# w_out's block sums in two buffer sets from their rows' landing; entry of the output stage by 256 tokens

## The reference

```python
h = _rmsnorm(x, g_pre)                                    # x: 1024 tokens x 1024
proj = einsum('bsd,dn->bsn', h, w_in)                     # q,k,v,z of A, q,k,v,z,lr of B, 2 gates
o_sb = stick_breaking(q, k, v)                            # A: 8 heads x 64, strictly causal
y_sb = (o_sb * silu(sb_z)) @ w_o_sb
log_alpha = log_sigmoid(gla_lr @ w_alpha_up + b_alpha_up) / 16
o_gla = _rmsnorm(gla_chunked(q, k, v, log_alpha), g_gla_norm)   # B: 4 heads
y_gla = (o_gla * silu(gla_z)) @ w_o_gla
merged = sigmoid(gA + bA) * y_sb + sigmoid(gB + bB) * y_gla
x = x + merged @ w_out
return _rmsnorm(x, g_final)
```

## Time and profile before

| | us |
|---|---|
| median of 3 runs | 827.39 |
| lowest, highest | 826.4, 827.99 |
| profiled execution | 827.49 |
| its span | 825.2 |
| PE busy | 795.7 (96%) |
| DVE busy | 585.2 (71%) |
| ACT busy | 410.1 (50%) |
| POOL busy | 54.7 (7%) |

### The profile page before, as it was taken

The page is one execution under the profiler, slowest core; times in us unless marked ns, Lnnn a source line. Parts: engine busy times, 40 slices in busy tenths (PEclk is TensorE's granted clock), DMA queues, the critical chain, the costliest instruction groups (busy, mean ns, idle before and its releaser), DMA issues.

```text
span 825.2 us, 11846 instructions
## 1 busy us (share of the span) xinstructions
PE 795.7 (96%) x4441; PEld 664.1 (80%) x4441; DVE 585.2 (71%) x807; ACT 410.1 (50%) x705; POOL 54.7 (7%) x44
## 2 busy tenths in 40 slices
PE   5989999999999999999999999999999999989996
PEld 4767888888788888879889888888888888868785
DVE  6776986989698888965545646566467777775884
ACT  8645665667566565756235245244344333353332
POOL 1550000000000000020000000000000000002510
PEclk9999999999999999999999999999999999999999
DMA  9794102202120220022111010244433334499232
GB/s 318 223 344 152 43 27 52 51 25 51 51 51 26 51 52 27 27 58 60 38 52 27 2 52 26 77 140 153 143 125 103 102 103 123 131 355 357 105 120 85
DMA packets 75171, 84.70 MB, mean 103 GB/s; under 512 B 3932, under 2 KB 57335, under 8 KB 74104
## 3 DMA queue, kind: packets, MB, share of 16 engines
q1 hardware_dynamic: 75074, 84.10, 31.5%
q10 hardware_dynamic: 54, 0.01, 0.0%
HBM read 59.98 MB, written 19.92 MB: 97 GB/s over the span
## 4 chain that ended last, share of the span: by engine, by line
PE 76%; DVE 12%; issue 4%; DMA 4%; ACT 3%; SPq 0%; DVEq 0%; ACTq 0%
PE pj L722 21%; PE ob L974 5%; PE sc L974 5%; PE tr L1026 4%; PE pj L866 4%; PE ob L1026 4%; DVE surv L1700 4%; PE pj L1026 4%; PE ob L814 3%; PE sc L1026 3%; PE tr L824 3%; PE pj L847 3%; PE pj L738 2%; PE sc L791 2%; PE sc L790 2%
## 5 line engine op out<-in xcount | busy, mean ns | idle before, releaser
L722 PE MATMUL pj<-h_hi,w_lo 128*128 128x512 f32 x336 | 134.6, 401 | 0.0
L722 PE MATMUL pj<-h_hi,w_hi 128*128 128x512 f32 x336 | 134.6, 400 | 0.0
L722 PE MATMUL pj<-h_lo,w_hi 128*128 128x512 f32 x336 | 134.3, 400 | 0.0
L1700 DVE TENSOR_TENSOR_SCAN surv<-surv 128x128 f32<-128x128 f32 (+3 forms) x64 | 86.4, 1350 | 24.1 <-ACT beta L1212 23.5
L722 PEld LDWEIGHTS pj<-h_hi,w_lo 128*128 128x128 f32 x336 | 63.9, 190 | 12.3 <-issue 0.5
L722 PEld LDWEIGHTS pj<-h_lo,w_hi 128*128 128x128 f32 x336 | 63.7, 190 | 12.2 <-issue 0.3
L722 PEld LDWEIGHTS pj<-h_hi,w_hi 128*128 128x128 f32 x336 | 63.9, 190 | 11.8 <-issue 0.2
L1253 ACT ACTIVATE wt_hi<-tr 128x512 fp32r<-128x512 f32 (+2 forms) x96 | 43.6, 490 | 43.3 <-PE tr L824 41.7
L1604 DVE TENSOR_TENSOR w_lo<-w_raw,w_hi 128x1024 fp32r<-128x1024 f32 x33 | 40.3, 1221 | 26.8 <-ACT w_hi L1124 26.6
L1745 DVE TENSOR_TENSOR wt_lo<-tr,wt_hi 128x512 fp32r<-128x512 f32 (+2 forms) x96 | 50.0, 548 | 5.3 <-ACT wt_hi L1253 4.8
L1703 DVE TENSOR_TENSOR beta<-beta,surv 128x128 f32<-128x128 f32 (+3 forms) x64 | 48.5, 758 | 2.2
(11 more groups left out here) (397 smaller groups left out, 1939.5 us busy)
## 6 DMA issues: line engine op xcount, KB each, us to landing
w_raw<-in_w_in SPq DMA_DIRECT2D x30, 512.0 KB, 3.7
tw<-w_scratch SPq DMA_DIRECT2D x8, 1024.0 KB, 9.2
y_scratch<-y_ring SPq DMA_DIRECT2D x28, 256.0 KB, 2.1
graw<-in_w_in SPq DMA_DIRECT2D x14, 512.0 KB, 5.2
y_back<-y_scratch SPq DMA_DIRECT2D x14, 512.0 KB, 5.2
x_t<-in_x SPq DMA_DIRECT2D x8, 512.0 KB, 6.6
wrow<-in_w_out SPq DMA_DIRECT2D x4, 1024.0 KB, 6.9
w_scratch<-wsum_h SPq DMA_DIRECT2D x4, 1024.0 KB, 7.6
```

What stands on the lines that cost most here:

```text
L722: mm = pe.matmul(pj[bank][:, :], (w_lo if p == 2 else w_hi)[:, slot, k, :], (h_lo if p == 1 else h_hi)[:, k, HALF * h:HALF * h + HALF], st ...
L1700: dve.tensor_tensor_scan(s[:, ::-1], s[:, ::-1], s[:, ::-1], 1.0, ALU.mult, ALU.bypass)\
```

## The change

In the opening the sums go round in two sets of places (k % 2) and each store has a semaphore of its own. POOL starts k = 0 with the landing of its rows, k = 2 waits for the store of k = 0's low part, and k = 3 for that of k = 1's. ACT's high part of k waits for the store of the high part of k - 2. ACT and DVE split all four before stage_k of c = 4 and before the stack; DVE's stack waits for the stores of the high parts of k = 1 and k = 3, and ACT and DVE enter the pairs when all eight are stored. All eight splits of h's first half stand before the split of k's weights. PE takes v's first half before the low-rank product, with the rounds of turns spread anew. The small loads of w_up go behind load 5.

At the output stage the last gate block is finished in two parts of 256 columns, and the first 256 tokens are merged, then both row blocks are split, then the rest is merged. The broadcast of g_final moves from before POOL's wait for the merge into its first pair, and DVE and ACT wait for it ahead of the first row sum and the first square. The norms of the pair before stand behind the third gather. g_fin_row lies elsewhere, and tw 3 is loaded ahead of x_res.

```diff
-        wsum = [at(f"wsum{k}", kb, [P, 4, HALF]) for k, kb in enumerate((F + 52, F + 68.125, F + 16, F + 52))]
-        wsum_h = [at(f"wsum_h{k}", kb, [P, 4, HALF], F32R) for k, kb in enumerate((F + 8, F + 40, F + 8, 108))]
-        wsum_l = [at(f"wsum_l{k}", kb, [P, 4, HALF], F32R)
-                  for k, kb in enumerate((F + 52, F + 68.125, F + 16, 100))]
+        wsum = [at("wsum0", F + 52, [P, 4, HALF]), at("wsum1", F + 68.125, [P, 4, HALF])]
+        wsum_h = [at("wsum_h0", F + 8, [P, 4, HALF], F32R), at("wsum_h1", F + 40, [P, 4, HALF], F32R)]
+        wsum_l = [at("wsum_l0", F + 52, [P, 4, HALF], F32R), at("wsum_l1", F + 68.125, [P, 4, HALF], F32R)]
...
             load(4, COL_Q + P, 0)
-            for c in range(8):
-                sp.dma_start(w_up[RANK * c:RANK * (c + 1), :], w_alpha_up[0]).then_inc(up_loaded, 16)
             load_wrow(2)
             load_wrow(3)
-            for k in range(3):
+            for k in range(4):
                 for part in range(2):
                     store_wsum(part, k)
             twin(0, 2)
             load(5, COL_K + P, 1)
-            for part in range(2):
-                store_wsum(part, 3)
-            for n, stores in enumerate((32, 32, 32, 16, 16)):
-                sp.wait_ge(wsum_stored[n], stores)
+            for c in range(8):
+                sp.dma_start(w_up[RANK * c:RANK * (c + 1), :], w_alpha_up[0]).then_inc(up_loaded, 16)
+            for n in range(2 * 4):
+                sp.wait_ge(wsum_stored[n], 16)
...
             load_tw(2)
-            sp.wait_ge(m_step, 3 * NP + 2)
-            load_res(0)
             sp.wait_ge(prod_done, NP * NP)
             load_tw(3)
+            sp.wait_ge(m_step, 3 * NP + 5)
+            load_res(0)
...
-            pool.wait_ge(x_normed, ST)
             for k in range(4):
                 top, low = wrow[k % 2][:, 0, :], wrow[k % 2][:, 1, :]
-                ts = wsum[k]
+                ts = wsum[k % 2]
                 pool.wait_ge(wrow_loaded[k % 2], 16 * (k // 2) + 16)
-                if k == 2:
-                    pool.wait_ge(tr_ready, R0)
-                if k == 3:
-                    pool.wait_ge(wsum_stored[0], 32)
+                if k >= 2:
+                    pool.wait_ge(wsum_stored[2 * k - 3], 16)
...
-            pool.wait_ge(fin_loaded, 16)
-            pool.partition_broadcast(g_fin[:, :], g_fin_row[0:1, :], P).then_inc(fin_bc, 1)
-
             pool.wait_ge(m_ready, 2)
-            pool.wait_ge(m_step, 3 * NP + 2)
+            pool.wait_ge(m_step, 3 * NP + 5)
...
                 if p == 1:
+                    pool.wait_ge(fin_loaded, 16)
+                    pool.partition_broadcast(g_fin[:, :], g_fin_row[0:1, :], P).then_inc(fin_bc, 1)
                     pool.wait_ge(o5_ready, 4)
...
             pe.wait_ge(cols_ready, 2)
             first_tile(0, 0, 0, [(7, 3)])
             first_tile(1, 1, 0, [])
+            first_tile(2, 2, 0, [(8, 4), (9, 6)])
             for k in range(KT):
-                turn_x([KT + k] if k < 3 else [])
+                turn_x([10 + k // 3] if k % 3 == 0 else [])
                 low_rank(0, k)
-            first_tile(2, 2, 0, [(11, 0), (12, 2), (13, 4), (14, 6)])
-            turn_x([15])
-            for n in range(2):
-                first_tile(n, 3 + n, 1, [])
+            first_tile(0, 3, 1, [(13, 0), (14, 1), (15, 3)])
+            first_tile(1, 4, 1, [])
             first_tile(2, 5, 1, [])
             for k in range(KT):
                 low_rank(1, k)
...
                 if o == 0 and p == 1:
-                    pe.wait_ge(comb, 5 * NP)
+                    pe.wait_ge(comb, 5 * NP + 1)
                     pe.wait_ge(sig_a, 2 * NP)
...
             def wsum_high(k, half):
 
                 hs = slice(2 * half, 2 * half + 2)
                 act.wait_ge(wsum_done, 4 * k + 4)
-                if k == 2:
-                    act.wait_ge(wsum_stored[0], 32)
-                act.activation(wsum_h[k][:, hs, :], wsum[k][:, hs, :], ACT.Copy).then_inc(wsum_hi, 1)
-
+                if k >= 2:
+                    act.wait_ge(wsum_stored[2 * k - 4], 16)
+                act.activation(wsum_h[k % 2][:, hs, :], wsum[k % 2][:, hs, :], ACT.Copy).then_inc(wsum_hi, 1)
+
+            for half in range(2):
+                wsum_high(0, half)
+            h_high(range(KT, KT + 2))
+            wsum_high(1, 0)
+            stage(v_t, 2, 0, 0)
+            wsum_high(1, 1)
+            h_high(range(KT + 2, KT + 5))
             lr_quarters(0)
-            h_high([KT + 3])
-            wsum_high(0, 0)
-            h_high([KT + 4])
-            wsum_high(0, 1)
             h_high(range(KT + 5, R0))
-            stage(v_t, 2, 0, 0)
             for half in range(2):
-                wsum_high(1, half)
+                wsum_high(2, half)
             stage(stage_q, 3, 1, 1)
             for half in range(2):
-                wsum_high(2, half)
+                wsum_high(3, half)
             stage(stage_k, 4, 1, 0)
             act.wait_ge(proj_free, 5)
-            act.wait_ge(wsum_stored[1], 32)
             for part in range(2):
                 stack(0, part)
             high_part(3, 1, 2, proj_ready, 5)
-            wsum_high(3, 0)
             stage(v_t, 5, 1, 1)
-            wsum_high(3, 1)
             lr_quarters(1)
-            act.wait_ge(wsum_lo, 8)
-            act.wait_ge(wsum_stored[2], 32)
-            act.wait_ge(wsum_stored[3], 16)
+            for n in range(2 * 4):
+                act.wait_ge(wsum_stored[n], 16)
...
                                bias=cols[:, 17 + v:18 + v]).then_inc(sig_b, 1)
+
+            def finish_part(part, done):
+
+                ps = slice(256 * part, 256 * part + 256)
+                act.wait_ge(comb, done)
+                act.activation(gates2[:, 1, ps], gates2[:, 1, ps], ACT.Sigmoid,
+                               bias=cols[:, 16 + NP:17 + NP]).then_inc(sig_b, 1)
 
...
-            finish_b(NP - 1)
+            finish_part(0, 5 * NP)
+            finish_part(1, 5 * NP + 1)
...
                     if o < 3:
                         act.wait_ge(prod_done, NP * NP)
-                        act.wait_ge(m_step, 3 * NP + 2)
+                        act.wait_ge(m_step, 3 * NP + 5)
                     if o == 3:
-                        act.wait_ge(fin_bc, 1)
+                        act.wait_ge(wout_l, 3)
...
             for o in range(4):
                 high_out(1, o)
+            act.wait_ge(fin_bc, 1)
             act.wait_ge(o5_free, 3)
             square(0, 0)
...
+            wsum_low(0, 0)
+            h_low(range(KT, KT + 2))
+            wsum_low(0, 1)
+            stage(v_t, 2, 0, 0)
+            wsum_low(1, 0)
+            h_low(range(KT + 2, KT + 5))
             lr_quarters(0)
-            h_low(range(KT + 3, KT + 5))
-            wsum_low(0, 0)
-            h_low([KT + 5])
-            wsum_low(0, 1)
-            h_low(range(KT + 6, R0))
-            stage(v_t, 2, 0, 0)
+            h_low(range(KT + 5, R0))
+            wsum_low(1, 1)
             for half in range(2):
-                wsum_low(1, half)
+                wsum_low(2, half)
             stage(stage_q, 3, 1, 1)
             for half in range(2):
-                wsum_low(2, half)
+                wsum_low(3, half)
             stage(stage_k, 4, 1, 0)
-            dve.wait_ge(wsum_stored[1], 32)
+            dve.wait_ge(wsum_stored[2], 16)
+            dve.wait_ge(wsum_stored[6], 16)
             for part in range(2):
                 stack(0, part, part)
             low_part(3, 1)
             stage(v_t, 5, 1, 1)
-            dve.wait_ge(proj_ready, 6)
-            for half in range(2):
-                wsum_low(3, half)
             lr_quarters(1)
-            dve.wait_ge(wsum_stored[2], 32)
-            dve.wait_ge(wsum_stored[3], 16)
+            for n in range(2 * 4):
+                dve.wait_ge(wsum_stored[n], 16)
...
-                dve.wait_ge(sig_a, 2 * v + 2)
-                dve.wait_ge(back_loaded, 32 * v + 32)
-                dve.tensor_tensor(mT[:, KT - 2 - v, :], s_a, y_back[:, 0, :], ALU.mult).then_inc(m_step, 1)
                 if v + 1 < NP:
+                    dve.wait_ge(sig_a, 2 * v + 2)
+                    dve.wait_ge(back_loaded, 32 * v + 32)
+                    dve.tensor_tensor(mT[:, KT - 2 - v, :], s_a, y_back[:, 0, :], ALU.mult).then_inc(m_step, 1)
                     low_item(v + 1, 5)
-                last_block(v)
-
-
-            def merge_last(h, done):
-
-                hs = slice(HALF * h, HALF * h + HALF)
-                dve.wait_ge(sig_b, 2 * NP - h)
-                dve.tensor_tensor(s_b[:, hs], s_b[:, hs], y_back[:, 1, hs], ALU.mult).then_inc(m_step, 1)
-                dve.wait_ge(m_step, 3 * NP - 2 + done)
-                dve.tensor_tensor(mT[:, 0, hs], mT[:, 0, hs], s_b[:, hs], ALU.add).then_inc(m_step, 1)
-
-            merge_last(1, 1)
-            merge_last(0, 3)
+                    last_block(v)
+
+
+            def last_part(part):
+
```

(78 more changed lines are left out.)

1 line of the change is left out of this document (removed).

## The result

| | before | changed |
|---|---|---|
| median, us | 827.15 (4 runs, 826.4 to 827.99) | 840.53 (4 runs, 839.8 to 841.45) |
| profiled execution, its span | 827.49, 825.2 | 841.45, 839.1 |
| PE busy | 795.7 | 800.1 |
| mean granted clock | 0.995 | 0.986 |
| first, second score on PE | 61.51, 68.30 | 73.52, 79.24 |

The ratio is 1.0162 (95% interval 1.0144 to 1.018): the change costs 13.4 us. The forecast was 832.6 with a range of 828 to 837. The sign was right and the size was not: 5.2 us were forecast.

The account below looks back on a forecast made before the run. PE was taken as the bound, busy 796 of 825 us, so only its waits, clock and new waits count. 827.5 plus 7.6 for the opening minus 2.4 for the output stage gave 832.7 (median 832.6), range 828 to 837.

Parts of the forecast that it names:

- Opening: Start to second score: two buffer sets chain sums behind stores, second score 75.9 instead of 68.3, +7.6 us.
- (1): Opening: POOL's third set waits for the first low part's store, landing about 46, and runs 46 to 51.2.
- (2): Opening: splits delay the second q half's copy; PE stands some 5 us before v's second half, off the last path.
- (3): Opening: POOL's fourth set waits for the second low part's store, landing at 51.2, and runs 51.3 to 58.1.
- (4): Opening: last high store lands at 65.1; its buffer lies on k_lo, so q and k low end at 67.4.
- (5): Opening: twin copies take 3.9 us, first score 71.3; 13 products at low clock, second score 75.9.
- Output stage, better part: Row blocks: merging 256 tokens first spares PE's wait for the second block, ending 743.4 instead of 748.70, -5.3 us.
- Output stage, worse part: Late broadcast's library switches, 7.3 us each, delay os2; block 4 begins at 769.1, leaving the output stage -2.4 us in all.
- B: Rival, output stage: switches are cheap or go under PE's row blocks; stage -6.2, time 828.9 us; chance 0.15.
- C: Rival, opening: stores take 8 us each and PE's clock stays low longer; 836.5 us; chance 0.17.
- D: Rival, opening: two buffer sets suffice, fourth set starts by 46, opening costs nothing; 823 us; chance 0.08.
- E: Rival, output stage: new order has no effect because c = 1 still waits; 838 us; chance 0.04.

Follow-up runs that it names:

- e12: Changed kernel with only the broadcast of g_final put back ahead of POOL's sums; ratio 1.005 to the kernel before, +4.1 us.
- e3: Kernel before with the changed output stage, but the broadcast of g_final early, ahead of POOL's sums; ratio 0.994, -5.0 us.
- e7: Changed opening with four buffer sets and the fourth set's splits behind the stacks, output stage of before; ratio 1.0039 to the kernel before, +3.2 us.
- e11: Kernel before with the changed output stage, g_final spread by its load instead of a POOL broadcast; ratio 0.9932, -5.6 us.
- e6b: Repeat run: changed opening with four buffer sets, output stage of before; ratio 1.0076 to the kernel before, +6.3 us.
- e1: Changed opening with the output stage of the kernel before; ratio 1.0138 to the kernel before, +11.4 us.
- e6: Changed opening with four buffer sets instead of two, output stage of before; ratio 1.0087 to the kernel before, +7.2 us.
- e1b: Changed opening with the old output stage, run again on another chip; ratio 1.0085 to the kernel before, +7.0 us.
- e4: Kernel before with only the broadcast of g_final moved late, between POOL's first two sums and os2; ratio 1.01, +8.3 us.

## Why the prediction was wrong

**Opening, forecast +7.6, profile +10.9, by e12 and e3 about +9.** The chain was the right one but for one link, and nearly every link came a little late:

| step of the prediction | forecast | measured |
|---|---|---|
| POOL's first set starts; sets end | 22.4; 29.4, 36.2 | 22.84; 29.7, 35.8 |
| v's first half on PE | 27.5 | 29.02 |
| first low store issued, landed (1) | 37, 46 | 38.54, 47.12 |
| third set ends (1) | 51.2 | 53.3 |
| PE's stand ahead of v's second half (2) | 5 us | 3.8 us |
| second low store issued (3) | 45.1 | 48.31 |
| fourth set (3) | 51.3 to 58.1 | 53.24 to 60.3 |
| last high store landed (4) | 65.1 | 66.62 |
| q and k low end (4) | 67.4 | 69.18 |
| first score (5) | 71.3 | 73.52 |
| 13 products and second score (5) | 75.9 | 79.24 |

Three terms of the sum were mis-sized. First, v's half: I took the time at which the old order had finished the tile before, plus a copy; in the trace it waited for DVE's copy of stage_q, which came at 28.50 behind the split of v's weights (2.31 us beside POOL) and the last row norm (1.56). That is 1.5 us, carried to the first low store, of which 1.1 is left at its landing. Second, each POOL set beside DVE's splits: the third took 6.0 us (47.3 to 53.3) for the 5.2 I had given it, and the fourth 7.1 for 6.8. Both engines have operations with two SBUF inputs there; I had charged DVE for it and POOL only in some steps. That makes 2.2 us at the end of the fourth set, and so late is the first score (behind it the last high store took 4.2 for my 5, the q and k low splits and the twin copies 0.7 more than I gave them). The one link that was another: in step 3 I let the second low store release the fourth set at 51.3; it landed at 52.3, and the fourth set began at 53.24 behind POOL's own third. The third term, 1.1 us, is PE's clock: I took 75.9 - 71.3 = 4.6 us from the first score to the second, because I had read that PE "ran 13 products with its clock at 0.50 of full". In the kernel before the clock was low only until 65.2, for some 3.4 of those 5 us, and with a wait of 4.5 us for k_lo ahead it was low until 78.2 in the changed one: 5.7 us. The sentence "none of this is last at the end of the opening", on the order at the start, was wrong in its consequence: in e7, with four buffer sets and the fourth set's splits at their old place, the new order at the start still costs 3.2 us.

**Output stage, better part, forecast -5.3 and (as a bound) -1.3: right.** Row blocks left 4.8 us earlier relative to the shift (766.07 - 11.3 = 754.8 against 759.6), and with the switches out of the way e3 and e11 gained 5.0 and 5.6 us.

**Output stage, worse part: the mechanism right, the size wrong.** Forecast was 19.8 us from POOL's first sum to os2 (740.8 to 760.6); measured 22.2 (752.71 to 774.94). I priced both switches by the one gap of 7.3 us. The one ahead was 5.6 and the one behind 10.95, and over the five traces with a late broadcast 5.5 to 9.2 and 10.3 to 12.0; and the two sums ahead took 0.4 more than I gave them. The step from os2 to block 4 was right (7.1 forecast, 7.2 measured). With the sums starting 0.6 us late, block 4 came at 783.46 - 11.3 = 772.2 and not at 769.1. What wasn't in the sum at all is PE's clock behind a wait of 6.3 us: 12 products in 5.20 and not 3.02, 2.2 us. -2.4 + 0.6 + 2.4 + 2.2 = 2.8, measured 2.6.

The bound of that term, "-1 if they cost a microsecond or two more", was too narrow for a duration of which one example was in the trace. Before the run, the 6 us that the Trainium skill gives for the first call to a freshly loaded kernel (GPSIMD Engine Reference, section 2.1) stood for a switch beside the 7.3; the gap ahead of the broadcast agrees with it in four of five traces (5.5 to 5.8), and the one behind is nearly twice as long. The working with it was wrong besides: two switches shorter by 1.3 each make 2.6 us, and I had written 1.5.

**The rivals.** B, cheap switches, falls: without them the stage gains (e3, e11), so its whole loss is theirs, with the clock behind the wait they cause. C had the right direction for both its parts: the clock, at half behind each stand, was in both mis-sized places. But its stores of 8 us weren't the cause (the last high store took 4.2, e6b loses 6.3 us with no store in the chain). D falls: the fourth set began at 53.24, not by 46. E falls: PE waited 0.2 us between the row blocks.

**Left open.** Why the clock differs between runs of one kernel (e1's at 0.983 or 0.992, 840 or 835 us); what two buffer sets cost by themselves, since e6 with four (7.2, 6.3) lies no lower than e1b with two (7.0) though its second score comes earlier; why the gap ahead was 9.2 us in e4 and its opening late; on what the length of the gap behind depends (6.8 to 8.2 with an early broadcast and the old output stage, 8.95 to 9.7 with an early one and the new stage, 10.3 to 12.0 with a late one).

A version that beats both kernels is e3, or e11 without the broadcast: the old opening, the first 256 tokens ahead, no switch in the open: 821.17 against 826.11 us, and 821.91 against 828.01.

## What to carry to other kernels

The partition broadcast had two prices here, one on each side, and both are hidden only in a wait that is longer than they are: look where POOL's queue behind it is next needed before moving it, or load the value already spread with a transfer. Where buffers are fewer, ask not only which store a set waits for but what is now queued ahead of the work that the next stage needs: here the splits ahead of the stack cost as much as the stores. And a new wait of PE of some microseconds cost, in most of these traces, its length and then products behind it at half clock (2.2 us at block 4), which belongs in the sum as a term of its own.

## What the runs showed of the hardware that wasn't expected

- The two gaps of POOL around a partition broadcast between its sums differ: 5.53, 5.62, 5.79, 5.80 and once 9.21 us ahead of it; 10.29, 10.95, 11.23, 11.44 and 11.96 behind it. With the broadcast in an idle stretch of POOL the next operation came 7.3 us behind it in the kernel before and 9.7 in e3, though its operands had been there for at least 3 us, and 6.8 to 9.7 in all twelve such traces.
- A DVE operation with two SBUF inputs is slowed in the same way by a broadcast: 1.35 for 0.42 us (128x256, e3 at 734.04), as the 2.23 of the earlier trace rows.
- Behind waits of PE of 2.4 to 7.4 us the clock was mostly at 0.50 for 3.4 or 6.8 us, in no strict order of their length: 3.3 us in e7 brought 6.8, 3.2 in the changed kernel 3.4. In e6b two waits in the opening (3.2 and 2.4 us) brought none, and two of 1.0 and 1.1 us around the second row block brought 3.4.
